# Keys and values of the recurrence turned as 32x32 squares on VectorE, each square carried to its place by a transfer inside SBUF

## The chip, the cores and the metric

The kernel runs on one core of a Trainium2 chip. The metric is the device time of one launch in microseconds (us), the median of several runs. All data are float32. The engines named below are TensorE (PE; its weight loads are shown apart as PEld), VectorE (DVE), ScalarE (ACT), GpSimd (POOL) and the queue engine SyncE (SP), which issues the DMA transfers here.

## The reference

The model is a two-layer block (feed-forward, a pooling and gated recurrence mixer, feed-forward) and then a second block with two mixers. The change lies in the first mixer of the second block, a linear recurrence over tokens with a matrix state per head. It is run over 512 tokens (256 of context, 256 of the input) in both directions, with 16 heads of 64:

```python
def wkv_scan(r, w, k, v, kk, a, s0, reverse):
    def step(S, inp):
        r_t, w_t, k_t, v_t, kk_t, a_t = inp
        sa = jnp.einsum("bhvk,bhk->bhv", S, kk_t)
        S = (S * w_t[:, :, None, :]
             - sa[..., None] * (kk_t * a_t)[:, :, None, :]
             + v_t[..., None] * k_t[:, :, None, :])
        return S, jnp.einsum("bhvk,bhk->bhv", S, r_t)
    s_fin, o = lax.scan(step, s0, xs, reverse=reverse)
```

## The kernel before

Features lie along the 128 partitions and tokens along the row. Weights stream from HBM through a ring of five slots of 1 MB, loaded by SP. After the first block and the projections of the second comes the recurrence, called the scan here, from about 1554 to 2047 us of the profiled span, and after it the output product, an attention mixer and the store.

The scan treats two heads at a time (a pair, 8 pairs, 128 features) and both directions at once. A pair has 8 steps of 64 tokens (`CHUNK`) in each direction. One **turn** q holds two steps in two directions, so four blocks u = (jj, d); a pair has four turns, named g = 0 to 3, and there are 32 turns. In a turn the products inside the blocks are computed (`first_gram`, `stacked_gram`), a 64x64 triangular matrix is inverted for each block by doubling in levels 1 to 5 (`lower_product` on PE, `mask_lower` on DVE, `next_inverse` on PE, `take_inverse` on ACT), and the state of the turn before is carried on with two steps k and k + 1, where k = 2(q - 1) (`state_product`, `take_z`, `solve`, `take_u`, `out_and_state`, `take_o`, `update_state`). Each engine has its own list of these steps, written out by hand in a loop over q, and executes it in order. Semaphores tie the lists together. The side work of a pair (norms, decays, gates) stands at fixed places of its turns, and POOL prepares the next pair meanwhile (`direction`).

Keys and values lie as feature by token. The state update and the output need them as token by feature. So in each turn PE transposes the four blocks of `bk` (128 rows each: 64 of betas and 64 of keys) in `turned_bk` (L1297) and four blocks of values in `turned_v` (L1315), into two PSUM banks; ACT copies these to `bk_t` and to the upper 64 partitions of `uv` (`take_turned_bk`, L1964, `take_turned_v`, L1969). The lower 64 partitions of `uv` are written by `take_u` (L1980). For the direction that runs backward ACT first writes a reversed copy of the values, `v_rev` (L1919), once for a pair. The readers are:

- the tile `kv` (L1369, in `side(q, "kv")`): values with the masked gram matrix, in turn q itself, which needs `uv`'s values of turn q;
- `out_and_state` (L1423, L1427, L1432), in turn q + 1 for the blocks of turn q, which needs `bk_t` and `uv`. Its last product counts up `os_full`.

`bk_t` and `uv` are double-buffered by the parity of q. The lines to follow in the trace: L1287 is `stacked_gram`, at whose first product a turn is counted here as begun; L1327 is `lower_product`, L1338 and L1340 are `next_inverse`, L1399 `state_product`, L1411 `solve`; on ACT L1957 and L1959 are `take_inverse`; on DVE L2763 is `mask_lower`, L2781 `take_z`, L2790, L2792 and L2793 `update_state`, L2753 to L2757 `begin_inverse`, L2697 `sum_decays`. On SP L976 are the weight loads before the scan, L993 those behind it and L996 the stores of the result. SP issues nothing between the load at the end of the projections and the first load for the output product.

## Time and profile before

| | |
|---|---|
| time of the kernel, median of 3 runs | 2393.3 us (2391.81 to 2393.4) |
| time of the profiled execution | 2391.25 us |
| its span in the profile | 2389.2 us |
| PE busy | 2357.6 us, 99% |
| DVE busy | 1526.6 us, 64% |
| ACT busy | 558.5 us, 23% |
| POOL busy | 419.0 us, 18% |
| first and last `stacked_gram` of the 32 turns | 1554.40 and 2035.73 us |

The profile is of one execution. Its span lies 2.05 us below that execution's time, and that time 2.05 us below the median. A row of a timeline says: start, duration, engine, line, operation, what is written and read, how many instructions are merged, and in brackets how long the engine sat idle before and whom it waited for. A float32 product shows as two matmul rows, so `x8` is four products. The granted clock of TensorE is 1.00 in all windows of the scan, its upper level of 2.4 GHz.

### The profile page before, as it was taken

How to read it: one execution, taken by the hardware profiler on the slowest of the kernel's cores; microseconds unless marked ns; L12 is line 12 of the kernel's file. 1: busy time of each engine (PE TensorE's matmuls, PEld its weight loads, DVE VectorE, ACT ScalarE, POOL GpSimd, SP SyncE). 2: the span in 40 equal slices, each digit the busy share in tenths (PEclk: the TensorE clock that was granted, in tenths of full speed). 3: DMA queues.
4: the chain of work that ended last, by engine and by line, in shares of the span. 5: the costliest groups of instructions: out<-in, count | busy, mean ns of one | idle time of the engine just before them, and what ended most of it. 6: DMA issues, size and time to landing. Idle time of an engine off the chain costs nothing.

```text
span 2389.2 us, 54476 instructions
## 1 busy us (share of the span) xinstructions
PE 2357.6 (99%) x24052; PEld 2057.5 (86%) x24052; DVE 1526.6 (64%) x2964; ACT 558.5 (23%) x1289; POOL 419.0 (18%) x483
## 2 busy tenths in 40 slices
PE   8999999999999999999999999999999999999999
PEld 8999888899999998889999888488888888556558
DVE  7886674488778766744987887255555554147652
ACT  2101030111011010301111111245555554132341
POOL 1111000112011100001223320234444440100000
PEclk9999999999999999999999999999999999999999
DMA  7555544445545554545454322000000001212111
GB/s 282 185 180 193 190 178 153 165 161 205 197 162 193 178 194 176 184 151 179 176 193 162 112 80 71 1 3 3 3 3 3 3 3 38 89 53 88 53 53 71
DMA packets 40427, 285.03 MB, mean 119 GB/s; under 512 B 4544, under 2 KB 5744, under 8 KB 6272
## 3 DMA queue, kind: packets, MB, share of 16 engines
q1 hardware_dynamic: 36000, 252.83, 29.6%
q0 software_dynamic: 4192, 28.72, 3.3%
q8 instruction: 190, 3.11, 0.5%
q14 instruction: 45, 0.37, 0.0%
HBM read 280.48 MB, written 1.05 MB: 118 GB/s over the span
## 4 chain that ended last, share of the span: by engine, by line
PE 96%; DVE 2%; ACT 2%; issue 0%; DMA 0%; POOL 0%; SPq 0%; DVEq 0%; ACTq 0%; POOLq 0%
PE psum L696 27%; PE psum L1039 21%; PE psum L1100 12%; PE psum L1208 6%; PE psum L714 5%; PE psum L1338 4%; PE psum L1327 3%; PE psum L1340 2%; PE psum L1287 1%; PE psum L1427 1%; ACT arena L1957 1%; PE psum L1010 1%; PE psum L1274 1%; PE psum L1297 1%; PE psum L1411 1%; PE psum L1355 1%
## 5 line engine op out<-in xcount | busy, mean ns | idle before, releaser
L696 PE MATMUL psum<-arena,ring 128*128 128x256 f32 (+1 forms) x2864 | 675.2, 395 | 8.3 <-ACT arena L1735 8.0
L696 PEld LDWEIGHTS psum<-arena,ring 128*128 128x128 f32 x2864 | 541.8, 190 | 129.7 <-issue 56.5
L1039 PE MATMUL psum<-arena 128*128 128x128 f32 x2560 | 325.0, 275 | 0.0
L1039 PEld LDWEIGHTS psum<-arena 128*128 128x128 f32 x2560 | 305.1, 192 | 0.0
L1039 PE MATMUL psum<-arena,ring 128*128 128x128 f32 x1920 | 253.6, 275 | 0.0
L1039 PEld LDWEIGHTS psum<-arena,ring 128*128 128x128 f32 x1920 | 233.9, 192 | 0.2
L2348 DVE TENSOR_TENSOR arena<-ring 128x1024 f32<-128x1024 f32 x136 | 171.1, 1258 | 38.6 <-PE psum L1100 34.7
L1100 PE MATMUL psum<-arena 128*128 128x128 f32 x1408 | 184.6, 275 | 0.0
L1100 PEld LDWEIGHTS psum<-arena 128*128 128x128 f32 x1408 | 170.7, 192 | 0.0
L2370 DVE SCALAR_TENSOR_TENSOR arena<-arena 128x256 f32<-128x256 f32 x336 | 164.1, 530 | 5.2
L1338 PE MATMUL psum<-arena 64*64 64x64 f32 x2560 | 158.5, 223 | 0.9 <-DVE arena L2763 0.7
L2763 DVE TENSOR_TENSOR arena<-psum,arena 128x256 f32<-128x256 f32 x160 | 67.8, 424 | 140.2 <-PE psum L1327 139.4
L1338 PEld LDWEIGHTS psum<-arena 64*64 64x64 f32 x2560 | 138.4, 133 | 13.5 <-issue 9.2
L1100 PE MATMUL psum<-arena,ring 128*128 128x128 f32 x1056 | 146.0, 275 | 0.0
L714 PE MATMUL psum<-arena,ring 128*128 128x512 f32 (+1 forms) x336 | 138.0, 555 | 1.1 <-DVE arena L2904 1.1
L1340 PE MATMUL psum<-arena 64*64 64x64 f32 x2048 | 131.9, 218 | 0.0
L1100 PEld LDWEIGHTS psum<-arena,ring 128*128 128x128 f32 x1056 | 131.5, 192 | 0.1
L1760 ACT ACTIVATE arena<-arena 128x256 f32<-128x256 f32 x88 | 36.8, 418 | 370.1 <-DVE arena L2486 343.7
L1327 PE MATMUL psum<-arena 64*64 64x64 f32 x2560 | 113.4, 221 | 9.0 <-ACT arena L1957 9.0
L1340 PEld LDWEIGHTS psum<-arena 64*64 64x64 f32 x2048 | 119.6, 135 | 0.0
L1327 PEld LDWEIGHTS psum<-arena 64*64 64x64 f32 x2560 | 94.8, 134 | 20.5 <-ACT arena L1957 13.7
L1957 ACT ACTIVATE arena<-psum 128x512 f32<-128x512 f32 x128 | 76.4, 597 | 147.6 <-PE psum L1340 147.6
(343 smaller groups left out, 3373.1 us busy)
## 6 DMA issues: line engine op xcount, KB each, us to landing
ring<-in_weights SPq DMA_DIRECT2D x238, 1024.0 KB, 4.8
arena<-in_ada POOLq DMA_DIRECT2D x24, 1024.0 KB, 5.4
arena<-in_const POOLq DMA_DIRECT2D x1, 1312.0 KB, 6.4
arena<-in_x SPq DMA_DIRECT2D x1, 1024.0 KB, 4.8
ring<-in_weights SPq DMA_DIRECT2D x2, 512.0 KB, 6.7
arena<-in_ctx POOLq DMA_DIRECT2D x1, 1024.0 KB, 7.5
arena<-in_lora POOLq DMA_DIRECT2D x1, 1024.0 KB, 5.2
out<-arena SPq DMA_DIRECT2D x8, 128.0 KB, 1.9
```

Of the source, the lines that this page charges most:

```text
L696: mm = self.nc.tensor.matmul(out, self.ring[:, slot % RING, i * P:(i + 1) * P], rhs, start=(kc == 0), stop=(kc == len(moving) - 1))
L714: mm = self.nc.tensor.matmul(out, self.ring[:, slot % RING, i * P:(i + 1) * P], rhs, start=start, stop=stop)
L1039: mm = nc.tensor.matmul(bank[:, n * P:(n + 1) * P], left[:, kind, pair, :], right[:, pair, :], start=(n == 0 and pair == 0), stop=(n == la ...
L1100: mm = nc.tensor.matmul(out_[name][:, n * P:(n + 1) * P], left[:, kind, place, :], right[:, pair, :], start=(n == 0 and pair == 0), stop=( ...
L1208: mm = nc.tensor.matmul(out_[:, n * T:(n + 1) * T], left[:, kind, pair, :], right[:, pair, :], start=(n == 0 and pair == 0), stop=(closes ...
L1327: mm = mm_(ps_t[b][halves[h], u, :], lt_all[halves[h], b, u, :], xy[halves[h], b, 0, u, :], start=True, stop=True)
L1338: mm = mm_(ps_xy[b][halves[h], 1, u, :], t_, y_, start=True, stop=True)
L1340: mm = mm_(ps_xy[b][halves[h], 0, u, :], y_, t_, start=True, stop=True)
L1957: ins = nc.scalar.activation(xy[:, b, :, :, :], ps_xy[b], ACT.Copy)
L2348: link(tt(sum_[:, S1:S3 + 1, :], w[:, W22:W11 + 1, :], w[:, W21:W21 + 1, :].to_broadcast([P, 2, QUADS * P]), ALU.add))
L2370: ins = stt(sum_, ada_[:, b, kc, :], weight, sum_, ALU.mult, ALU.add)
L2763: tt(t_low[:, b, :, :], ps_t[b], mask(f"below{level}"), ALU.mult).then_inc(s.t_masked[b], 1)
```

## The change

`turned_bk`, `turned_v` and their copies on ACT go, and `reverse_values` with its buffer. In their place DVE turns squares of 32x32 within a row of partitions (`turn_squares`), and SP carries each row of squares with a transfer from SBUF to SBUF to the partitions where it belongs. For this the layout of `bk_t` and `uv` changes: the block index u is now innermost, so that one partition's row of a square (32 columns, 4 blocks) is contiguous, 512 bytes; every reader and `take_u` now step over four elements (16 bytes) along the features. The reversed direction is read with a negative step. One buffer `squares_turned` holds six groups of squares, four for `bk` and two for the values.

```diff
-    bk_t = second.take(2, 4, P)
-    uv = second.take(2, 4, P)
+    bk_t = second.take(2, P, 4)
+    uv = second.take(2, P, 4)
+    squares_turned = Arena(arena, second.at).take(6, SQUARE, 4)
...
+            for q in range(TURNS):
+                b, n = q % 2, q // 2 + 1
+                if q >= 2:
+                    sp.wait_ge(s.bk_landed[b], 16 * 16 * (n - 1))
+                    sp.wait_ge(s.v_landed[b], 8 * 16 * (n - 1))
+                sp.wait_ge(s.squares_turned, q + 1)
+                if q >= 2:
+                    sp.wait_ge(s.os_full, 2 * q - 2)
+                for c in range(6):
+                    rows = slice(c % 4 * SQUARE + c // 4 * CHUNK, c % 4 * SQUARE + c // 4 * CHUNK + SQUARE)
+                    dst, landed = (bk_t, s.bk_landed) if c < 4 else (uv, s.v_landed)
+                    for f in range(P // SQUARE):
+                        cols = slice(f * SQUARE, (f + 1) * SQUARE)
+                        sp.dma_start(dst[rows, b, cols, :], squares_turned[cols, c, :, :]).then_inc(landed[b], 16)
+                for i in range(2):
+                    if q == TURNS - GROUPS + 1 + i:
+                        load_b(i)
+            for i in range(2, SECOND_B_SLOTS):
+                load_b(i)
...
                     if kind == "kv":
                         pe.wait_ge(s.gram_taken, q + 1)
-                        pe.wait_ge(s.act_taken, SCAN.taken(("v_turned", q)))
+                        pe.wait_ge(s.v_landed[q % 2], 8 * 16 * (q // 2 + 1))
...
-                                         uv[HEAD:P, q % 2, u, h * HEAD:(h + 1) * HEAD], start=True, stop=True)
+                                         uv[HEAD:P, q % 2, h * HEAD:(h + 1) * HEAD, u], start=True, stop=True)
...
                 pe.wait_ge(s.u_taken, k + 1)
+                if jj == 0:
+                    pe.wait_ge(s.bk_landed[par], 16 * 16 * (q // 2 + 1))
...
-                        mm = mm_(ps_s[halves[h], d, :], bk_t[:, par, 2 * jj + d, cols], uv[:, par, 2 * jj + d, cols],
+                        mm = mm_(ps_s[halves[h], d, :], bk_t[:, par, cols, 2 * jj + d], uv[:, par, cols, 2 * jj + d],
...
                 next_inverse(q, 3)
-                turned_bk(q)
-                turned_v(q)
                 lower_product(q, 4)
...
+            def turn_squares(q):
+                pair, g = divmod(q, GROUPS)
+                if g == 0:
+                    dve.wait_ge(s.pair_ready, pairs_ready(pair, 1))
+                if q >= 1:
+                    dve.wait_ge(s.bk_landed[(q - 1) % 2], 16 * 16 * ((q - 1) // 2 + 1))
+                    dve.wait_ge(s.v_landed[(q - 1) % 2], 8 * 16 * ((q - 1) // 2 + 1))
+                stream, at = g // 2, g % 2 * 2 * CHUNK
+                for d in range(2):
+                    nc.vector.transpose(
+                        squares_turned[:, 0:4, :, d::2].rearrange("p c j u -> p u c j"),
+                        bk[:, pair % 2, d, 2 * g:2 * g + 2, :].rearrange("p u (c j) -> p u c j", j=SQUARE))
+                    values = rkv[:, 2 * DC + pair, stream * T:(stream + 1) * T]
+                    values = (values if d == 0 else values[:, ::-1])[:, at:at + 2 * CHUNK]
+                    ins = nc.vector.transpose(
+                        squares_turned[:, 4:6, :, d::2].rearrange("p c j u -> p u c j"),
+                        values.rearrange("p (u c j) -> p u c j", u=2, c=2))
+                ins.then_inc(s.squares_turned, 1)
...
             begin_inverse(1)
+            dve.wait_ge(s.lora_in, 4)
+            turn_squares(0)
...
                 if q % GROUPS == 0 and q // GROUPS + 1 < PAIRS:
                     sum_decays(q // GROUPS + 1)
+                elif ahead:
+                    turn_squares(q + 1)
                 if ahead:
                     mask_lower(q + 1, 2)
                 if k >= 0:
                     update_state(k + 1)
+                if q % GROUPS == 0 and q // GROUPS + 1 < PAIRS:
+                    turn_squares(q + 1)
```

PE, turn 5 (the second turn of the second pair), from the end of level 3 to the first step of the state. Before: L1340 is the end of `next_inverse`, L1297 and L1315 the two transposes, L1327 `lower_product`, L1423 the start of `out_and_state`.

```order
L1340 MATMUL psum<-arena 64x64
L1297 MATMUL psum<-arena,ring 128x128 [waits act_taken]
L1297 MATMUL psum<-arena,ring 128x128 x3
L1315 MATMUL psum<-arena 128x128 [waits act_taken]
L1315 MATMUL psum<-arena,ring 128x128
L1315 MATMUL psum<-arena 128x128
L1315 MATMUL psum<-arena,ring 128x128
L1327 MATMUL psum<-arena 64x64 [waits xy_taken_1]
L1327 MATMUL psum<-arena 64x64 x7
L1423 MATMUL psum<-ring,arena 64x64 [waits u_taken]
L1423 MATMUL psum<-ring,arena 64x64 x3
```

The same place after the change. Its line numbers are those of the changed kernel: L1342 is `next_inverse`, L1329 `lower_product`, L1427, L1431 and L1436 are `out_and_state`.

```order
L1342 MATMUL psum<-arena 64x64
L1329 MATMUL psum<-arena 64x64 [waits xy_taken_1]
L1329 MATMUL psum<-arena 64x64 x7
L1427 MATMUL psum<-ring,arena 64x64 [waits bk_landed_0,u_taken]
L1427 MATMUL psum<-ring,arena 64x64 x3
L1431 MATMUL psum<-arena 64x64 x4
L1436 MATMUL psum<-arena 64x64 x4
```

The eight transposes are gone, `lower_product` stands directly behind `next_inverse`, and `out_and_state` waits for the keys' transfers as well.

DVE, the second half of turn 5. Before: L2763 is `mask_lower`, L2781 `take_z(k + 1)`, L2792 and L2793 `update_state(k + 1)`.

```order
L2763 TENSOR_TENSOR arena<-psum,arena 128x256 [waits t_full_1]
L2781 TENSOR_TENSOR arena<-psum,arena 128x128 [waits z_full]
L2763 TENSOR_TENSOR arena<-psum,arena 128x256 [waits t_full_0]
L2792 TENSOR_TENSOR arena<-psum,arena 128x128 [waits o_taken]
L2793 TENSOR_TENSOR arena<-arena 128x128 [waits dve_chain]
```

The same place after the change; L2750 and L2755 turn the squares of turn 6.

```order
L2764 TENSOR_TENSOR arena<-psum,arena 128x256 [waits t_full_1]
L2782 TENSOR_TENSOR arena<-psum,arena 128x128 [waits z_full]
L2750 STREAM_TRANSPOSE arena<-ring 128x2x128 [waits v_landed_1,bk_landed_1]
L2755 STREAM_TRANSPOSE arena<-arena 128x2x64
L2750 STREAM_TRANSPOSE arena<-ring 128x2x128
L2755 STREAM_TRANSPOSE arena<-arena 128x2x64
L2764 TENSOR_TENSOR arena<-psum,arena 128x256 [waits t_full_0]
L2793 TENSOR_TENSOR arena<-psum,arena 128x128 [waits o_taken]
L2794 TENSOR_TENSOR arena<-arena 128x128 [waits dve_chain]
```

Four transposes stand between `take_z` and the next `mask_lower`, and wait until all transfers of turn 5 have landed. In turns with g = 0 they stand behind `update_state(k + 1)` instead.

SP, after the change, from the first loads through two turns of the scan; L980 are the weight loads, L1017 the new transfers of 32 partitions by 128 elements. Before, the load of the first slot behind the scan follows directly on the `x214`.

```order
L980 DMA ring<-in_weights 128x2048 [waits slot_used] x214
L1017 DMA arena<-arena 32x128 [waits squares_turned]
L1017 DMA arena<-arena 32x128 x23
L1017 DMA arena<-arena 32x128 [waits squares_turned]
L1017 DMA arena<-arena 32x128 x23
L1017 DMA arena<-arena 32x128 [waits squares_turned,os_full,v_landed_0,bk_landed_0]
L1017 DMA arena<-arena 32x128 x23
```

Each of the 32 turns has 24 transfers in a row; from turn 2 on the first of them waits for `os_full`, which guards the buffer that is written over.

## Rows read from the trace of the kernel before

**Rows 1.** The page, busy time by engine and the chain that ended last.

```profile
PE 2357.6 (99%) x24052; PEld 2057.5 (86%) x24052; DVE 1526.6 (64%) x2964; ACT 558.5 (23%) x1289; POOL 419.0 (18%) x483
...
PE 96%; DVE 2%; ACT 2%; issue 0%; DMA 0%; POOL 0%; SPq 0%; DVEq 0%; ACTq 0%; POOLq 0%
```

**Rows 2.** Windows, turns 4 to 7: us, then busy PE, PEld, DVE, ACT, POOL.

```profile
1615.34:1631.23 15.89, 15.67 (x399) 13.91 (x396) 9.41 (x19) 8.41 (x19) 1.27 (x1) 1.00 0.01 3
1631.23:1647.31 16.08, 15.86 (x384) 13.45 (x381) 8.75 (x19) 9.18 (x22) 13.33 (x12) 1.00 0.02 4
1647.31:1662.35 15.04, 14.79 (x387) 13.81 (x384) 8.29 (x17) 6.97 (x16) 9.06 (x7) 1.00 0.02 4
1662.35:1678.25 15.90, 15.68 (x399) 13.92 (x396) 7.70 (x19) 7.09 (x16) 4.12 (x3) 1.00 0.01 3
sum 62.91, PE 62.00 PEld 55.08 DVE 34.16 ACT 31.66 POOL 27.78; mean PE 15.50 PEld 13.77 DVE 8.54 ACT 7.92 POOL 6.95
```

**Rows 3.** Timeline of turn 5 around the transposes: start, duration, engine.

```profile
1633.68 0.66 PE L1297 MATMUL psum<-arena,ring 128*128 128x128 f32 x4
...
1634.71 0.68 PE L1327 MATMUL psum<-arena 64*64 64x64 f32 x16
...
1633.79 0.60 ACT L1957 ACTIVATE arena<-psum 128x512 f32<-128x512 f32 x1 [0.22 <-PE psum L1340]
```

**Rows 4.** Waits of PE in the scan: us in total, times, longest.

```profile
PE psum L1327 <- ACT arena L1957: 9.0, 34, 0.8
```

**Rows 5.** Timeline of DVE, turns 3 to 6, the gaps and three durations.

```profile
1612.08 0.29 DVE L2793 TENSOR_TENSOR arena<-arena 128x128 f32<-128x128 f32 x1
...
1627.71 0.17 DVE L2790 MEMSET arena<- 128x128 f32 x1 [0.77 <-ACT arena L1992]
1630.87 0.29 DVE L2781 TENSOR_TENSOR arena<-psum,arena 128x128 f32<-128x128 f32 x1 [3.00 <-PE psum L1399]
...
1633.34 0.42 DVE L2757 TENSOR_TENSOR arena<-arena 128x256 f32<-128x256 f32 x1
...
1642.56 0.42 DVE L2763 TENSOR_TENSOR arena<-psum,arena 128x256 f32<-128x256 f32 x1 [2.10 <-PE psum L1327]
...
1649.86 1.50 DVE L2757 TENSOR_TENSOR arena<-arena 128x256 f32<-128x256 f32 x1
```

**Rows 6.** Timeline of PE in turn 5, readers of the turned tiles.

```profile
1635.55 0.45 PE L1427 MATMUL psum<-arena 128*64 128x64 f32 x8
1635.83 0.40 PE L1432 MATMUL psum<-arena 128*64 128x64 f32 x8
1636.17 1.12 PE L1387 MATMUL psum<-arena 128*128 128x512 f32 x2
...
1641.27 0.27 PE L1369 MATMUL psum<-arena 64*64 64x64 f32 x1
...
1641.69 0.27 PE L1327 MATMUL psum<-arena 64*64 64x64 f32 x1
...
1643.30 0.34 PE L1338 MATMUL psum<-arena 64*64 64x64 f32 x4
```

**Rows 7.** SP's issues: timeline at the start; durations in ns; landing in us.

```profile
2.78 1.99 SPq L976 DMA_DIRECT2D ring<-in_weights  x4
...
L976 SPq DMA_DIRECT2D ring<-in_weights x214: 327/328/1092, 2.8 to 1475.0; - x107
...
L996 SPq DMA_DIRECT2D out<-arena x8: 332/340/456, 2371.8 to 2386.9; - x8
...
DMA to landing us min/median/max: 1.9/1.9/4.0
```

**Rows 8.** Timeline of turn 0, DVE and PE.

```profile
1553.78 0.42 DVE L2757 TENSOR_TENSOR arena<-arena 128x256 f32<-128x256 f32 x1
...
1555.49 0.34 PE L1338 MATMUL psum<-arena 64*64 64x64 f32 x4
...
1564.86 0.27 PE L1369 MATMUL psum<-arena 64*64 64x64 f32 x1
```

More of the change, by code:

```diff
@@ L89 @@
 STACK_BANKS = (2, 5)
+SQUARE = 32
 DA_HEADS = 8
@@ L405 @@
 SECOND_A = second_a_order()
-PLACES = ("bk_turned", "v_turned", "middle", "kv", "end")
+PLACES = ("middle", "kv", "end")
 def scan_tiles(q, place):
@@ L414, in scan_tiles @@
     inside, ahead, behind = 0 <= pair < PAIRS, pair + 1 < PAIRS, pair >= 1
-    if place in ("bk_turned", "v_turned", "kv"):
+    if place == "kv":
         return [(place, q, "act")] if inside else []
@@ L583, in __init__ @@
         self.y_ready = new("y_ready")
-        self.reversed_ready = new("reversed_ready")
+        self.squares_turned = new("squares_turned")
+        self.bk_landed = [new(f"bk_landed_{b}") for b in range(2)]
+        self.v_landed = [new(f"v_landed_{b}") for b in range(2)]
         self.out_squared = new("out_squared")
@@ L838, in build @@
     bk, ar = by_pair[:, :, 0], by_pair[:, :, 1]
-    v_rev = v_part.take(2, CHUNK + T2)
     prod = v_part.take(STEPS, CHUNK + 1), second.take(STEPS, CHUNK + 1)
@@ L976, in _, with load_b @@
                 sp.dma_start(ring[:, r, :], weights[i]).then_inc(s.slot_landed[r], 16)
-            sp.wait_ge(s.slot_used, RING_AT_REST)
-            for i in range(SECOND_B_SLOTS):
+            def load_b(i):
                 r = (RING_SHIFT + i) % RING
                 if i == 0:
-                    sp.wait_ge(s.act_taken, SCAN.taken(("bk_turned", TURNS - GROUPS - 1)))
+                    sp.wait_ge(s.slot_used, RING_AT_REST)
+                    sp.wait_ge(s.squares_turned, TURNS - GROUPS)
+                    sp.wait_ge(s.stack_full, TURNS - GROUPS)
                 elif i == 1:
@@ L985, in _ @@
                 elif i == 2:
-                    sp.wait_ge(s.act_taken, SCAN.taken(("bk_turned", TURNS - 1)))
+                    sp.wait_ge(s.squares_turned, TURNS)
+                    sp.wait_ge(s.stack_full, TURNS)
                 elif i == 3:
@@ L989, in _ @@
                 elif i == 4:
-                    sp.wait_ge(s.act_taken, SCAN.taken(("v_turned", TURNS - 1)))
+                    sp.wait_ge(s.pair_ready, pairs_ready(PAIRS - 1, 1))
                 else:
@@ L1426, in out_and_state @@
                     for h in range(2):
-                        mm_(ps_o[halves[h], d, :], uv[:, par, 2 * jj + d, h * HEAD:(h + 1) * HEAD],
+                        mm_(ps_o[halves[h], d, :], uv[:, par, h * HEAD:(h + 1) * HEAD, 2 * jj + d],
                             gram_at(par, jj, d, h)[:, CHUNK:], start=False, stop=True)
@@ L1924, in side_head @@
                 n = pair + 1
-                if g == 0 and n < PAIRS:
-                    reverse_values(n)
                 if g == 1 and n < PAIRS:
```

42 lines of the change are left out of this document (1 added, 41 removed).

## The prediction, made before the changed kernel ran

> **What bounds the kernel now.** I read the page's busy times and chain first. PE is busy 99% of the span and holds 96% of the chain [rows 1], so a change pays only where it shortens PE's row of work or costs where it makes PE wait. Then the windows of four turns, one pair of the scan: PE is busy 15.50 of 15.73 us in a mean turn, DVE 8.54, ACT 7.92, POOL 6.95 [rows 2]. The turns last 15.89, 16.08, 15.04 and 15.90 us. DVE and ACT have room, but the room lies in gaps. PE's waits in the scan are small: 9.0 us in all on `take_inverse` [rows 4]. Last the timelines around the places that the change touches.
>
> **PE's transposes, removed.** In turn 5 the first transpose starts at 1633.68 and `lower_product` of level 4 at 1634.71, so eight transposes take 1.03 us [rows 3]. They are not worth 1.03 us, since they cover a wait: `lower_product` needs ACT's `take_inverse`, which runs from 1633.79 to 1634.39. PE follows such a release by about 0.05 us, so the product starts at 1634.44, which is 0.27 us earlier. What is late next is thus ACT's copy. For the 31 turns after the first that is 31 x 0.27 = 8.4 us. The copies on ACT (about 1.2 us in a turn) and the reversed values go as well; ACT is idle there, so they count as nothing.
>
> **DVE's transposes, added.** A turn adds two of 256 and two of 128 elements a partition. No transpose stands in the trace. The nearest rows are element by element operations inside SBUF, 0.42 us for 256 and 0.29 us for 128 [rows 5], so 2 x (0.42 + 0.29) = 1.42 us; I take this, and twice it, 2.84, as the upper bound. A faster one gains nothing, as they are hidden. In turns with g = 1 to 3 they stand in the gap of 2.10 us before `mask_lower` at 1642.56, in those with g = 0 behind the `MEMSET` at 1627.71, ahead of a gap of 3.00 us [rows 5]. Both hold 1.42 us. At 2.84 us the first gap is 0.74 us too short; the mask's reader, `next_inverse`, starts at 1643.30, 0.32 us after the mask ends, so 0.4 us is left in 24 turns, 10 us. POOL's work next door can do the same: one 256-element operation took 1.50 us instead of 0.42 [rows 5].
>
> **SP's transfers, added.** 24 issues in a row and a landing. The trace has no transfer of 32 rows. Issues of 128 rows take 0.33 us each, alone [rows 7]; four back to back at the start take 1.99 us, 0.50 each. The last store needs 1.9 us from issue to landing. I take 0.41 us between two issues, the middle, as a quarter of the rows should not be dearer than 128: 23 x 0.41 + 1.9 = 11.3 us, and 0.1 us for the wake-up makes 11.4. The bounds are 23 x 0.33 + 2.0 = 9.6 and 23 x 0.50 + 2.0 = 13.5 us.
>
> The time available is read from two places. In a turn with g = 0 the squares are ready at 1627.71 + 0.17 + 1.42 = 1629.30, and `kv` (L1369), which needs the values, which are issued last, starts at 1641.27 [rows 5, 6]; less the 0.27 us gained that is 11.7 us. In the other turns SP waits for `os_full`, the end of `out_and_state(k + 1)`, that is about 1643.30, not for the squares; from there to the next `kv` is a turn less 2.03 us (1643.30 - 1641.27). With the shortest usual turn, 15.04 - 0.27, it is 12.7 us. So 11.4 us fits both, by 0.3 us in the first. DVE's next transposes want the landing about 0.8 us before `kv` does; the gap's spare 0.68 us takes most of that. Queued behind a late landing on DVE would be `mask_lower(q + 1, 2)` and `update_state`; behind a late one on PE all of the scan.
>
> **Once, at the start.** `turn_squares(0)` stands between `begin_inverse(1)`, done at 1554.20, and `mask_lower(0, 3)`. The latter then ends at 1554.20 + 1.42 + 0.43 = 1556.05, and `next_inverse`, at 1555.49 before, starts 0.6 us late. The transfers land at 1554.20 + 1.42 + 11.4 = 1567.0, and `kv` of turn 0 started at 1564.86 [rows 8]. This costs 2.2 us in all, once; bounds 0.4 and 4.3 us by the two prices of the transfers. The loads for the output product are issued later, behind the squares of turns 29 to 31, but the first is needed only after the scan; I cost this at nothing.
>
> **Strided reads, changed.** `kv` reads `uv`, and the last two products of `out_and_state` read `uv` and `bk_t`, over a step of 16 bytes. In time on PE these are 0.42 us (1641.27 to 1641.69) and twice 0.28 + 0.34 us (1635.55, 1635.83, 1636.17) [rows 6], 1.66 us in a turn. No row has an operand with a step, apart from tiny ones. The lower bound is no cost (the rows as they are), the upper a doubling, 1.66 x 32 = 53 us. The nearest row is the same product with a step of one, so I take nothing, and keep 53 us for a rival. `take_u` writes with this step too: 0.42 us for two copies, on ACT, which has room.
>
> This is the one place where the Trainium skill speaks against the change. Its page "SBUF — State Buffer", section "Door 1: The DMA port swizzle", says that SBUF has lines of 16 bytes, that at least two hits on a line are needed for full bandwidth, and yet that four float32 can be stepped over for free. Taken by its first half each read here meets a new line; taken by its second it costs nothing. No run here shows it. The page "DMA: Bandwidth & Descriptors", section "Bandwidth", calls transfers under 64 KB dominated by descriptors; these have 16 KB.
>
> **The sum.** -8.4 + 2.2 = -6.2 us. The profiled execution of 2391.25 us becomes 2385.0; against the median, 2.05 us higher, 2387.1. I forecast 2387.0 us.
>
> **Rivals.**
>
> 1. *SP can't issue fast enough.* The scan then follows a new ring: 24 transfers, `kv`, `out_and_state`, `os_full`, 24 transfers. For it: the four back-to-back issues at 0.50 us. Against: an issue alone takes 0.33 us. At 0.50 us the 13.5 us miss the 11.7 us after each g = 0 by 1.8, and the 12.7 us of the short turn by 0.8: 2.6 x 8 pairs = 21 us, at the start 4.3 instead of 2.2, so -8.4 + 21 + 4.3 = +17 us, 2410. It costs from 0.42 us on, since 23 x 0.42 + 2.0 = 11.7, and by about 0.44 us it has eaten the gain. At 0.65 us a turn needs 16.95 + 2.03 = 19.0 us, and the total would be near 2510.
>
> 2. *The strided operands are read slowly.* -6.2 + 53 = +47, 2440 us; at half that price 2414. It decides from 0.2 us in a turn on. It needs no queue to fail, since PE has nothing to hide it behind; for it speaks that these reads were all packed before, against it only that a float32 product of 64 columns is no faster than its neighbours. The skill's line rule, first half, is this rival; by its second half it falls.
>
> 3. *DVE's squares are dearer*, by themselves or beside POOL, which works 13.33 of 16.08 us in a turn with g = 1 [rows 2]: -6.2 + 10 = +4, 2397 us.
>
> 4. *The gain is larger*, if the freed 1.03 us could be used in full: only if ACT's copy were not the next wait, which row and order exclude.
>
> **Chances.** The forecast, with covers that hold, 40%: its own range is 2384 to 2395. Rival 1, 23%; rival 2, 28%; rival 3, 9%. A measurement of this kernel can tell about 0.2%, 4.8 us, from no change. Of the forecast's 40%, 31 lie below 2388.5 and 9 within; rivals 1 and 3 bring 8 more within, and 1 for a lucky case below. So faster 0.32, same 0.17, slower 0.51: the likeliest single case is a small gain, but the cases on the other side hold more together. The range reaches over rival 2 and most of rival 1: 2383 to 2450. It leaves out a deeper failure of SP's pace (12%) and a few per cent below.
>
> **What would show it.** Right: no L1297 and L1315; the turns of a pair 0.27 us shorter; the groups of `kv` and `out_and_state` with the same spacing; SP's issues at 0.41 us or less; DVE's four transposes 1.42 us and no wait for a DMA on PE. Rival 1: PE's waits name the new transfers, all turns equally long, SP busy through. Rival 2: PE busy as before, but 0.28 and 0.34 us of L1427 and L1432 grown, and the loads too, with no wait behind it. Rival 3: DVE's transposes over 2.1 us, or PE waiting for `mask_lower`. What would make the prediction wrong at once is a pace above 0.42 us or any price on the step of 16 bytes.

## The result and the profile after

The changed kernel takes **2623.09 us** (median, 2621.86 to 2624.62), the kernel before 2393.35: a ratio of 1.0965, 95% interval 1.0952 to 1.0978. The forecast was 2387.0, a small gain, with a range from 2383 to 2450. The kernel became slower instead, and its time lies 236 us above the forecast.

The page comes first: busy times, the granted clock over 40 slices, and each engine's part in the chain that ended last.

```profile
PE 2428.3 (93%) x23796; PEld 2119.7 (81%) x23796; DVE 1568.1 (60%) x3091; ACT 531.0 (20%) x1217; POOL 416.4 (16%) x483
...
PEclk9999999999999999999999998888888888899999
...
PE 74%; SPq 18%; DMA 2%; issue 2%; DVE 2%; ACT 1%; POOL 0%; DVEq 0%; ACTq 0%; POOLq 0%
```

PE had 96% of the chain [rows 1] and now has 74%; of the 22 points that it lost, 18 went to SP's queue (SPq). The clock row falls in the slices of the scan only (the eights). The next rows are the windows of turns 4 to 7, to be held against [rows 2]. A row gives the length in us, then the busy time of PE, PEld, DVE, ACT and POOL, the granted clock, the DMA share and GB/s:

```profile
1646.25:1668.12 21.87, 17.13 (x391) 15.26 (x388) 10.96 (x23) 7.18 (x16) 1.28 (x1) 0.92 0.08 18
1668.12:1693.72 25.60, 18.63 (x376) 15.74 (x373) 10.32 (x23) 8.43 (x20) 21.93 (x18) 0.80 0.09 21
1693.72:1715.31 21.59, 16.49 (x379) 15.43 (x376) 8.52 (x21) 6.24 (x14) 0.00 (x0) 0.92 0.09 19
1715.31:1738.85 23.54, 17.81 (x391) 15.94 (x389) 9.26 (x23) 6.35 (x14) 4.11 (x3) 0.85 0.09 20
```

Four turns last 92.60 us, where they were 62.91. Over all 32, from the first `stacked_gram` (1553.80) to the last (2256.74), a turn has 22.68 us in the mean, against 15.53 before. That is 31 x 7.15 = 222 of the 230 us; most of the rest lies in the last turn and the last steps of the state behind it. DMA works 8 to 9% of the time, so the engines that move the bytes are not what is short.

Next the waits in the scan (us in total, how often, the longest), first of PE, whose largest was 9.0 us before [rows 4], and of DVE, then of SP:

```profile
PE psum L1371 <- DMA arena<-arena: 137.3, 31, 7.3
DVE arena L2750 <- DMA arena<-arena: 131.7, 24, 7.2
...
SPq L1008 <- DVE arena L2755: 111.3, 30, 7.0
...
SPq L1011 <- PE psum L1436: 46.9, 24, 2.1
```

PE's `kv` (L1371) and DVE's next squares (L2750) wait for the landing, and SP waits for DVE's squares and for PE's `out_and_state` (L1436) before it may issue again: a ring. One passage of it in turn 6, from the timeline (start, duration, engine, line, what; in brackets the idle time before and what ended it):

```profile
1707.48 0.64 DVE L2750 STREAM_TRANSPOSE arena<-ring 128x256 f32<-128x256 f32 x1 [5.34 <-DMA arena<-arena]
1707.49 0.67 PEld L1371 LDWEIGHTS psum<-arena 64*64 64x64 f32 x12 [4.30 <-issue]
1707.52 0.78 PE L1371 MATMUL psum<-arena 64*64 64x64 f32 x10 [4.19 <-DMA arena<-arena]
...
1709.87 0.75 PE L1431 MATMUL psum<-arena 128*64 128x64 f32 x8
...
1710.40 0.69 PE L1436 MATMUL psum<-arena 128*64 128x64 f32 x8
```

And SP's issues of L1017 (durations in ns, minimum, median, maximum; under it the time to landing):

```profile
L1017 SPq DMA_DIRECT2D arena<-arena x768: 507/591/1880, 1555.1 to 2269.4; - x192
...
DMA to landing us min/median/max: 1.7/1.8/3.7
```

From the starts of the 768 issues: within a row of 24, two neighbours lie 0.633 us apart in the median, 0.717 in the mean. So the first and the last of 24 lie 16.50 us apart in the mean; 1.85 us later the last has landed, and 4.16 us after that SP issues the next row's first (the way back). The sum, 22.5 us, is the turn. The window that the forecast read from the trace of before was 11.7 us.

The way back is not the same in all turns. In six turns with g = 0, where DVE's squares stand behind `update_state` and SP waits for them, it is 5.6 to 5.9 us. In the usual other turns it is 3.85 us, with a granted clock of 0.50 (the lower level, 1.2 GHz) from the landing to the next issue. In the two turns where the clock was 1.00 there, it is 3.21 us. Two such stretches, both from turns with g = 3, from the last landing to SP's next issue:

```profile
2002.12:2005.97 3.85, 3.71 (x59) 3.51 (x61) 1.98 (x5) 0.44 (x2) 0.00 (x0) 0.50 0.00 0
1911.72:1914.93 3.21, 3.21 (x74) 3.04 (x71) 2.02 (x5) 1.55 (x6) 1.23 (x1) 1.00 0.01 3
```

So the usual way back is 0.64 us longer at the lower clock. Whether the clock fell because PE waits is asked further down.

### The profile page after: what moved, and what is told of

It is laid out like the page before. It is cut to its first block, busy times and chain, and to the rows that moved or that the text cites. A ratio compares the mean times of both kernels' runs of the same rounds, so it can differ in the third digit from the quotient of the medians.

```text
span 2619.8 us, 54905 instructions
## 1 busy us (share of the span) xinstructions
PE 2428.3 (93%) x23796; PEld 2119.7 (81%) x23796; DVE 1568.1 (60%) x3091; ACT 531.0 (20%) x1217; POOL 416.4 (16%) x483
## 4 chain that ended last, share of the span: by engine, by line
PE 74%; SPq 18%; DMA 2%; issue 2%; DVE 2%; ACT 1%; POOL 0%; DVEq 0%; ACTq 0%; POOLq 0%
PE psum L699 25%; PE psum L1068 19%; SPq L1017 18%; PE psum L1129 11%; PE psum L1237 5%; PE psum L717 5%; DMA arena<-arena 2%; PE psum L1371 1%; PE psum L1329 1%; PE psum L1039 1%; PE psum L1427 1%; PE psum L1431 1%; PE psum L1589 1%; PE psum L1631 1%; PE psum L1436 1%
## 5 line engine op out<-in xcount | busy, mean ns | idle before, releaser
L1340 PE MATMUL psum<-arena 64*64 64x64 f32 x2560 | 174.6, 236 | 0.9 <-DVE arena L2764 0.9
L1371 PE MATMUL psum<-arena 64*64 64x64 f32 x512 | 37.1, 297 | 137.3 <-DMA arena<-arena 137.3
L1340 PEld LDWEIGHTS psum<-arena 64*64 64x64 f32 x2560 | 150.6, 143 | 15.7 <-issue 9.9
L1329 PE MATMUL psum<-arena 64*64 64x64 f32 x2560 | 132.5, 236 | 31.5 <-ACT arena L1952 31.5
L1342 PE MATMUL psum<-arena 64*64 64x64 f32 x2048 | 146.7, 233 | 0.0
L1329 PEld LDWEIGHTS psum<-arena 64*64 64x64 f32 x2560 | 112.1, 147 | 41.9 <-ACT arena L1952 39.5
L1371 PEld LDWEIGHTS psum<-arena 64*64 64x64 f32 x512 | 31.1, 186 | 140.7 <-issue 140.7
L1342 PEld LDWEIGHTS psum<-arena 64*64 64x64 f32 x2048 | 131.9, 149 | 0.0
```

The source lines that it names most:

```text
L1329: mm = mm_(ps_t[b][halves[h], u, :], lt_all[halves[h], b, u, :], xy[halves[h], b, 0, u, :], start=True, stop=True)
L1340: mm = mm_(ps_xy[b][halves[h], 1, u, :], t_, y_, start=True, stop=True)
L1342: mm = mm_(ps_xy[b][halves[h], 0, u, :], y_, t_, start=True, stop=True)
L1371: mm = mm_(out_[halves[h], u * HEAD:(u + 1) * HEAD], gram_at(q % 2, jj, d, h)[HEAD:P, 0:CHUNK], uv[HEAD:P, q % 2, h * HEAD:(h + 1) * HEAD, ...
```

## Experiments

All ratios are to the kernel before, run on the same chip beside each (2391.4 to 2392.2 us).

**One part of the change at a time.** First the layout alone, in the kernel before:

```diff
-    bk_t = second.take(2, 4, P)
-    uv = second.take(2, 4, P)
+    bk_t = second.take(2, P, 4)
+    uv = second.take(2, P, 4)
...
-    uv[HEAD:P, q % 2, u, h * HEAD:(h + 1) * HEAD]
+    uv[HEAD:P, q % 2, h * HEAD:(h + 1) * HEAD, u]
```

> The kernel before, with one part of the change alone: the buffers bk_t and uv are laid out with the four units innermost, so that PE reads them, and ACT writes them, over a step of 16 bytes. The transposes stay on PE, and no transfers are added. Theory A, that SP's transfers alone lengthened the turn from 15.5 to 22.7 us and that the granted clock fell as a consequence: the time stays within 5 us of 2393, since the step costs nothing. Theory B, that the step has a price of its own: in the trace of the changed kernel the three groups of reads were wider than before (about 0.16 us each for the first two products of the output, 0.14 for the third, 0.1 to 0.2 for kv, twice or once a turn), which makes 0.8 to 1.2 us in a turn and 25 to 40 us in 32, so 2418 to 2433 us, with PE busy throughout and the granted clock at 1.00. Theory C, that the step is most of the loss and the transfers only wait for a slower PE: over 2500 us.

Measured: **2441.91 us**, 1.0213 (1.0196 to 1.0230), so +50.5 us. Theory B had the mechanism, but its 25 to 40 us were too low. The groups of the three readers (busy us, mean ns of one), first of the kernel before, then of this one:

```profile
L1427 PE MATMUL psum<-arena 128*64 128x64 f32 x512 | 28.9, 234 | 0.0
...
L1432 PE MATMUL psum<-arena 128*64 128x64 f32 x512 | 25.8, 222 | 0.0
L1369 PE MATMUL psum<-arena 64*64 64x64 f32 x512 | 25.4, 221 | 0.1
```

```profile
L1427 PE MATMUL psum<-arena 128*64 128x64 f32 x512 | 44.3, 294 | 0.0
L1432 PE MATMUL psum<-arena 128*64 128x64 f32 x512 | 44.0, 305 | 0.0
L1369 PE MATMUL psum<-arena 64*64 64x64 f32 x512 | 40.1, 293 | 0.0
```

15.4 + 18.2 + 14.7 = 48.3 us, nearly all of it. PE stays 99% busy, and no wait of PE grows by more than 0.2 us in total: this cost doesn't show as a wait.

Then the whole change with half of its transfers (`for f in range(0, P // SQUARE, 2)`, and the counts that are waited for halved):

> The changed kernel with 12 transfers to a turn in place of 24: half of the squares are not moved, so half of the turned keys and values are left out; everything else, DVE's transposes and the step of 16 bytes too, is as changed. Theory A, SP's pace: the measured mean of 0.72 us from issue to issue makes 11 x 0.72 + 1.8 = 9.7 us for 12, which fits the 11.7 us that the shortest window holds, so the ring of transfers and products opens; the turns fall from 22.7 to 15.3 us plus the price of the step (0 to 1.2 us), the total is between 2385 and 2425 us, the granted clock in the scan returns to 1.00, and PE's wait for the transfers (137 us) is nearly gone. Rival: the transfers are late because of where they start (the wait for the output product and the landing), not because of how many they are: then a turn loses only what it gains in the middle, and stays above 18 us, over 2470 us in all.

Measured: **2434.80 us**, 1.0180 (1.0165 to 1.0196). The usual turns of a pair are 17.14, 17.31, 16.19 and 17.14 us, where the kernel with the step alone has 17.41, 17.57, 16.46 and 17.41: in each 0.27 us less, which is the gain that the forecast read from [rows 3]. The granted clock is 1.00 in the four windows of these turns. The first:

```profile
1619.17:1636.31 17.14, 16.23 (x391) 14.54 (x389) 10.96 (x23) 7.18 (x16) 1.29 (x1) 1.00 0.06 12
```

Taken away in this order, the parts are: the step +50.5, PE's transposes removed and the first dozen of transfers added -7.1 (2434.80 less 2441.91), and the second dozen of transfers +188.3 us. Each is the difference of two neighbouring runs, so that they add up to the whole by construction. Another order gives other parts, as the packed kernel further down shows.

> The changed kernel with 18 transfers to a turn (a quarter of the squares is not moved, and that part of the turned keys and values is left out). With 24 a turn takes 22.7 us, with 12 the ring is open and a turn takes 17.1 (of which 1.5 are the step, as the kernel before with the step alone showed). Theory A, a ring of SP's issues at a mean 0.72 us each: the turn is 22.7 - 6 x 0.72 = 18.4 us, so 31 x (18.4 - 17.14) = 39 us over the kernel with 12, about 2474 us, and up to 15 us less if the granted clock recovers; the point at which it stops to cost lies at 16 to 17 transfers. Rival, a threshold instead of a line (the lower granted clock is what makes the turn long, and it is either there or not): the time is either that of 12, 2435, or over 2550 us.

Measured: **2498.90 us**, 1.0448 (1.0434 to 1.0462). It is not the one value or the other of the rival: the time lies between, but 25 us above the expected 2474. From SP's issues: first to last 12.03 us (17 x 0.71, as expected), the last landing 2.68 us later in place of 1.85, then 4.07, together 18.8 us. What the expectation left out is that the landing of the last transfer can be late too, 2.9 to 3.7 us in 17 of 32 turns; with 24 transfers it was late in one. Six turns have the length that they have with 12 transfers (17.14 or 16.2 us), so there the transfers came in time.

**What an issue costs.** The block of spare transfers, in the kernel before:

```diff
+            def square_moved(i):
+                sp.dma_start(there[rows(i % 4), cols(i // 4)], here[rows(i // 4), cols(i % 4)]).then_inc(s.tried, 16)
...
+            def from_hbm(i):
+                sp.dma_start(there[rows(i % 4), cols(i // 4)], weights[i][rows(i % 4), cols(i // 4)]).then_inc(s.tried, 16)
```

> The kernel before, with spare transfers issued by SP in the turns 1 to 27 of the scan, whose data nobody reads; nine forms in blocks of three turns, 16 issues back to back in a turn (4 for the widest form), each form on a source line of its own: a square of 32 rows by 512 bytes to other rows and to the same rows, a short one of 32 rows by 128 bytes, 128 rows by 128 bytes, 128 rows by 512 bytes, 32 rows by 512 bytes from HBM, 128 rows by 128 bytes from HBM, 32 rows by 512 bytes to HBM, and 16 rows by 1 KB. Theory A, the price of an issue depends on where its source and destination lie: from SBUF to SBUF about 0.59 us whatever its size, from HBM about 0.33 us with 0.50 back to back, as at the start of the kernel before. Theory B, it grows with the number of pieces: 128 rows cost clearly over 32 rows of the same form. Theory C, crossing from rows to other rows costs more than staying on the same rows. In every case the kernel's own time stays within 15 us of 2393, as SP is idle in the scan, and PE's granted clock at 1.00.

Measured: 2392.02 us in one run, with a granted clock of 1.00 in the scan, so the spare transfers cost the kernel nothing. Theory A holds, with 0.42 us for HBM back to back in place of 0.50. The forms (ns, as above): a square to other rows (L992), a square on its rows (L995), 128 rows by 128 bytes (L1001), 128 rows by 512 bytes (L1004), a square from HBM (L1007), to HBM (L1013).

```profile
L992 SPq DMA_DIRECT2D arena<-arena x48: 507/591/1539, 1571.7 to 1611.9; - x48
...
L995 SPq DMA_DIRECT2D arena<-arena x48: 507/591/1738, 1616.1 to 1659.0; - x48
...
L1001 SPq DMA_DIRECT2D arena<-arena x48: 464/602/1692, 1710.9 to 1753.0; - x48
...
L1004 SPq DMA_DIRECT2D arena<-arena x12: 464/601/602, 1757.8 to 1790.7; - x12
...
L1007 SPq DMA_DIRECT2D arena<-in_weights x48: 310/422/1895, 1804.8 to 1845.7; - x48
...
L1013 SPq DMA_DIRECT2D scratch_out<-arena x48: 302/422/1449, 1899.6 to 1939.3; - x48
```

Inside SBUF, rows, bytes and whether partitions are crossed change next to nothing (a square of 4 KB 0.59 us, 128 rows of 64 KB 0.60). What counts is whether one end lies in HBM (0.42) or none (0.59).

> The changed kernel with the buffers bk_t and uv packed again, as in the kernel before, so that PE reads without a step; the same 24 transfers to a turn, each in runs of 128 bytes in place of 512 (128 pieces of 128 bytes, 16 KB as before), and DVE's transposes write packed. Theory A, the ring is SP's issues: it still holds, and loses only the price of the step that lies in it (kv and one output product, 0.2 to 0.8 us a turn): 2595 to 2620 us, if an issue costs the same for four times as many pieces. Theory B, an issue is paid by its pieces: 0.59 us becomes well over 1 us, a turn over 35 us, over 3000 us in all. Theory C, the step is the main cause: below 2500 us.

Measured: **2624.05 us**, 1.0974 (1.0958 to 1.0991). Four times as many pieces cost an issue 602 ns in place of 591. Theory A holds in its mechanism, not in its size: the packed reads should have shortened the ring, but the time is the changed kernel's. SP's first to last grew to 16.81 us (0.3 lost) and the rest fell to 5.8 us, 3.90 and 1.87 (0.2 won).

The way back tells why so little was won. Where the granted clock is 0.50 it is 3.68 us in a usual turn, against 3.85 with the step: there the step costs only 0.17 us. Where the clock is 1.00, in two turns, it is 2.24 us against 3.21:

```profile
2187.51:2189.75 2.24, 2.10 (x61) 2.00 (x63) 1.58 (x5) 0.44 (x2) 0.00 (x0) 1.00 0.00 0
```

So in the changed kernel the step's 50 us do not come on top of the ring: without the step, the 24 direct transfers alone make it as slow.

The longest issues stood out. In the changed kernel 83 took over 0.9 us, and all of them overlap in time with a packet of 16 KB from an instruction queue, itself 0.9 to 1.5 us long; of the 685 shorter ones 79 do. In the scan there are 93 such packets (packets, MB, share):

```profile
q8 instruction: 93, 1.52, 0.9%
```

That is only a coincidence in a trace, so the same transfers were run where no other engine works:

> The kernel before, and behind its last store, where no other engine works, four blocks of 48 transfers of 32 rows by 512 bytes each, of which nobody reads the data: SP from SBUF to SBUF, SP from HBM to SBUF, ACT's queue from SBUF to SBUF alone, then SP's and ACT's both at once. Theory A, the long issues (1.0 to 1.9 us, 2 to 3 in a turn of the scan) come from PE's instruction fetches: here no issue is over 0.7 us and the mean start to start is 0.63 us, 0.46 for HBM. Rival, they belong to SP's own queue: as many long ones as in the scan, 6 or 7 in 48, mean 0.70 to 0.75. On both at once, theory B: each queue keeps 0.63 us, so that two queues halve the time of 24 transfers; rival: they share one path and each slows to 1.2 us. The whole adds 48 x (0.63 + 0.46 + 0.63 + 0.63) + 8 = 121 us, 2510 us in all.

The kernel took 2514.41 us in one run, where 2510 were expected. The 48 issues of each block (L2159 has two blocks), and below them the packets of the instruction queue in the whole stretch:

```profile
L1005 SPq DMA_DIRECT2D ring<-ring x48: 586/590/592, 2392.4 to 2422.2; - x48
...
L1008 SPq DMA_DIRECT2D ring<-in_weights x48: 310/421/442, 2423.9 to 2445.9; - x48
...
L1012 SPq DMA_DIRECT2D ring<-ring x48: 518/599/828, 2479.9 to 2510.2; - x48
...
L2159 ACTq DMA_DIRECT2D ring<-ring x96: 515/612/613, 2447.7 to 2509.9; - x96
...
q14 instruction: 2, 0.02, 0.0%
```

The median is that of the scan, and the long ones are gone (592 ns at most against 1539). So they come from what the other engines do in the scan. The instruction packets are the one traffic found beside them; no run took these away alone, so that they are the cause is likely and not shown. The mean start to start is 0.633 us, against 0.717 in the scan: the long ones add 23 x 0.084 = 1.9 us to a turn. SP's and ACT's queues at once (L1012 with the second half of L2159) keep 0.64 us each, so the price belongs to the issuing queue.

**Is it the number of issues?** If so, fewer and cheaper ones do away with the 188 us, though the bytes are moved twice, out to HBM in 8 transfers and back in 2:

```diff
-                        sp.dma_start(dst[rows, b, cols, :], squares_turned[cols, c, :, :]).then_inc(landed[b], 16)
+                    sp.dma_start(v_out[b, :, cols, :].rearrange("(c i) j u -> i c j u", c=2), squares_turned[cols, 4:6, :, :])
...
+                sp.dma_start(uv[CHUNK:P, b, :, :], v_out[b]).then_inc(s.v_landed[b], 16)
```

> The changed kernel with DVE's transposes and the step of 16 bytes as changed, but the squares go to a buffer in HBM in 8 stores to a turn (32 rows each, pieces of 512 bytes) and from there to bk_t and uv in 2 loads: 10 issues in place of 24, all with one end in HBM, which in the block of spare transfers took 0.42 us each back to back against 0.59 from SBUF to SBUF. Theory A, the number of issues and their price make the ring: stores 8 x 0.46 = 3.7, landing 1.6, loads 0.9 and 2.0, together 8.2 us, fit the window, so the time is that of the kernel with 12 transfers, 2430 to 2440 us (the step's 50 us less the 8.4 us of PE's removed transposes). Rival, the bytes and pieces make it (twice the traffic): the wait of PE for the load stays, over 2500 us.

Measured: **2434.72 us**, 1.0177 (1.0163 to 1.0191), to 0.1 us the time of the kernel with 12 transfers, and with all of the data. In its scan neither PE nor DVE waits for a transfer. One more thing differs: SP starts the 8 stores without waiting for `os_full`, since they don't write over `bk_t` and `uv`, and DVE waits for the stores alone. That part of the ring is open whatever the count, so this run does not separate the number of issues from where they start. The kernel with 12 transfers does: it keeps the starting point, and its ring opens because the transfers are fewer. Now the step too is taken away, with 4 stores and 6 loads:

> As the kernel by way of HBM, but with bk_t and uv packed as in the kernel before, so that PE and ACT work without the step: 4 stores to a turn (32 rows, 768 pieces of 128 bytes each, 96 KB) and 6 loads (32 rows, 128 pieces of 512 bytes, 64 KB). Theory A, both causes taken away leave the change's gain: 2391.4 - 8.4 + 1 to 3 us once at the start = 2384 to 2386 us, the turns of a pair 0.27 us shorter than before. Rival 1, the small pieces are slow: 3072 pieces of 128 bytes to a turn need more than the 11.7 us window together with the loads; then PE waits for the loads and the time is over 2400 us. Rival 2, DVE's transposes of 2.0 us cost something of their own: 2388 to 2400 us without a wait for a transfer on PE.

Measured: **2389.28 us**, 0.9988 (0.9979 to 0.9997): a small gain, 4 us short of Theory A. Against the packed kernel with 24 direct transfers (2624.05) it is 235 us: in this order the transfers cost all and the step nothing. Its turns tell why 4 us are missing. Most are 0.27 us shorter, as 15.63 for 15.90. Those with g = 2 are 15.27 for 15.04, and turn 1 is 17.19 for 15.65. In the turns with g = 2, PE now waits for DVE's mask (L2763 before, L2767 here). The waits for it in the whole scan, before and after:

```profile
PE psum L1338 <- DVE arena L2763: 0.7, 1, 0.7
```

```profile
PE psum L1344 <- DVE arena L2767: 4.1, 8, 0.7
```

In turn 1 a single wait of 1.76 us for ACT, which loads a table there (the wait was 0.74 us before), is followed by five microseconds at a granted clock of 0.66, a stretch partly at the lower level of 1.2 GHz; the two wide products in it take 2.08 us in place of 1.12:

```profile
1570.69:1575.00 4.31, 2.55 (x61) 2.29 (x58) 2.98 (x6) 4.17 (x8) 0.75 (x1) 1.00 0.34 65
1575.00:1580.00 5.00, 5.00 (x73) 3.31 (x75) 2.56 (x5) 1.53 (x4) 4.81 (x5) 0.66 0.19 57
```

The first of the two, the wait for the mask, has a cure:

```diff
-                mask_stack(q, 0)
-                mask_lower(q, 4)
+                if q % GROUPS == 2:
+                    mask_lower(q, 4)
+                    mask_stack(q, 0)
+                else:
+                    mask_stack(q, 0)
+                    mask_lower(q, 4)
```

> The packed kernel by way of HBM with one change of DVE's order: in the turns with g = 2 mask_lower of level 4 stands ahead of the first mask_stack, not behind it. There POOL's work slows begin_inverse (1.36 and 1.49 us in place of 0.69 and 0.42), so that the mask ended at 1653.13 and PE waited 0.52 us for it, in 8 turns 4.1 us in all; in the kernel before PE's eight transposes covered this wait, so the gain of 0.27 us in a turn became a loss of 0.23 in these turns (15.04 to 15.27 us). Theory A: the mask's place is the cause. It starts 0.6 us earlier, the wait goes, these turns fall to 14.8 us and the time by about 4 us, to 2385 us, 0.3% under the kernel before. Rival: the wait only moves to mask_stack's readers or to update_state, and the time stays at 2389.

Measured: **2385.15 us**, 0.9970 (0.9959 to 0.9982); the usual turns with g = 2 fall to 14.69 us, and of the 8 waits one is left, which the kernel before has too. This version is faster than both kernels, than the one before by 7 us, 0.3%.

**DVE's part, and the step's size.**

> The kernel before with DVE's four transposes of a turn added, at the places of the changed kernel and into a packed buffer that nobody reads; PE's transposes and ACT's copies stay. It asks for the price of DVE's part alone. Theory A, hidden in DVE's gaps, as forecast: 2391 to 2393 us, with 0.42 and 0.27 us for the two kinds (1.4 us in a turn), plus at most 0.6 us once at the start. Rival, it delays mask_lower in the turns where POOL works beside DVE: 2395 to 2405 us, and PE's waits name L2763's line with several us.

Measured: **2391.64 us**, 0.9999 (0.9990 to 1.0008). The squares are hidden here, where nothing waits for their landing; 28 of the 32 turns have them. With a packed output they take 413 and 269 ns, 1.36 us in a turn; in the changed kernel, where they write over the step, 627 and 392, or 2.04.

> The kernel before with bk_t and uv laid out over a step of 8 bytes (two units innermost) in place of 16, for PE's reads and ACT's writes alike; nothing else is changed. The step of 16 bytes cost 50.5 us. Theory A, that what counts is how many of the operand's elements lie in one line of 16 bytes (the Trainium skill, page SBUF - State Buffer, section Door 1: The DMA port swizzle, holds two hits on a line to be enough): no cost, 2391 us. Theory B, any step but one costs the same: 2442 us. Theory C, the cost grows with the step: between, about 2415.

Measured: **2395.13 us**, 1.0011 (1.0002 to 1.0020), +2.9 us. PE's three means are 237, 224 and 222 ns, 1 to 3 ns more than packed; ACT's copy of 512 elements is 636 ns, where it was 596 packed and 1099 over 16 bytes. So nearly all of the price comes between 8 and 16 bytes; 12 were not tried. The Trainium skill (SBUF — State Buffer, Door 1: The DMA port swizzle) asks for at least two hits on a line of 16 bytes for full bandwidth, and with that the trace agrees; its reading that four float32 can be stepped over for free is refuted here by 50 us.

> The kernel before with the step of 16 bytes in bk_t alone, which is the stationary operand of one of the three groups (L1432) and is written by one of ACT's copies; uv stays packed. With both stepped that group's product rose from 222 to 305 ns in the mean and the three groups cost 15.4, 18.2 and 14.7 us. Theory A, one stepped operand of a product costs as much as two, whichever it is: 15 to 18 us, 2407 to 2410 us. Theory B, the two operands add up: 8 to 10 us, 2400 to 2402. Theory C, a stepped stationary operand is hidden behind the product before it: within 3 us of 2392.

Measured: **2408.02 us**, 1.0065 (1.0050 to 1.0080), +15.8 us, Theory A. The group L1432 goes from 25.8 us to 41.1 with one stepped operand and to 44.0 with two; the prices of two operands of one product don't add up.

**The clock.** It fell to 0.80 to 0.92 in the changed kernel's turns. Is it the cause of the long turns or a consequence? PE gets products that nobody reads, ahead of its wait:

```diff
+                        for i in range(FILLERS):
+                            filler = gram_at(q % 2, 0, 0, 0)[HEAD:P, 0:CHUNK]
+                            mm_(out_[halves[i % 2], 0:HEAD], filler, filler, start=True, stop=True)
                         pe.wait_ge(s.v_landed[q % 2], 8 * 16 * (q // 2 + 1))
```

> The changed kernel, with 128 small products on PE in each turn ahead of its wait for the transfers, written to the tile of kv, which the real products overwrite: about 3.4 us in a turn, while PE waited 4.4 us there in the mean. The granted clock in the scan was 0.86. Theory A, the lower clock follows from PE's waits and costs little by itself, since the ring is SP's: the clock rises towards 1.00, and the time stays between 2600 and 2640 us. Rival, the lower clock is what makes the turns long: with it back at 1.00 the time falls below 2560 us.

Measured: **2678.63 us**, 1.1197 (1.1182 to 1.1213), clock 1.00, usual turns of 24.6 us. No theory met this: I had mis-sized the filling, 7.5 us in a turn and not 3.4, so that PE was the bound (96% busy in the scan). Repeated with 60:

> The changed kernel with 60 in place of 128 small products on PE in each turn ahead of its wait for the transfers. The 128 took 7.5 us in a turn (24.6 against 17.1), 58 ns each, so that PE and not SP was the bound, and that run says nothing of the clock's price; 60 are 3.5 us, and PE's work in a turn 20.6 us, under the ring's 22.5. Theory A, the lower clock (0.86) follows from PE's waits and costs little: the clock rises to 0.95 or more, the turn stays within 0.6 us of 22.6, the time between 2600 and 2640 us. Rival, the lower clock makes up 1.5 us or more of the 5.6 us that a turn is longer than with 12 transfers: with the clock back the time falls to 2575 us or less. A second rival, more instructions on PE mean more fetches that hold SP's issues up: the time rises by the same share as the long issues, to 2650 us.

Measured: **2636.80 us**, 1.1032 (1.1014 to 1.1051). The clock rose, but less than expected. The same 690 us of the scan and 100 us of it, first of the changed kernel, then of this one:

```profile
1560.00:2250.00 690.00, 527.72 (x11469) 470.07 (x11469) 291.74 (x672) 212.05 (x470) 187.61 (x151) 0.87 0.09 22
1660.00:1760.00 100.00, 77.28 (x1665) 68.57 (x1667) 41.14 (x97) 31.91 (x70) 28.60 (x23) 0.86 0.08 18
```

```profile
1560.00:2250.00 690.00, 613.20 (x14940) 558.04 (x14942) 289.65 (x666) 210.60 (x465) 187.69 (x151) 0.92 0.09 22
1660.00:1760.00 100.00, 91.08 (x2286) 82.60 (x2284) 43.97 (x100) 31.90 (x71) 28.68 (x23) 0.97 0.09 20
```

So the clock follows PE's waits: it is 1.00 with 128 products and 0.92 in the scan with 60. But the mean from one row of issues to the next is 22.8 us, for 22.5, and nothing speaks for the rival in which the clock makes up 1.5 us or more of a turn. The way back shows its size directly. In this run too it is 3.7 to 3.8 us in the usual turns at the lower level and 3.1 in six turns where the clock was higher (three more of these were longer, for reasons not found), so the clock is worth some 0.6 us a turn. By an estimate from the two rows of the changed kernel, 31 x 0.64, that is up to 20 us of its 230. Here the gain of a few turns doesn't show in the time. The last landing came 2.19 us behind its issue in place of 1.85, and 32 x 0.34 = 11 us is as much as the 10.4 us between the spans of the two profiled executions. There were 141 packets of the instruction queues for 111, which fits the second rival in direction.

## Why the prediction was wrong, by its steps

- **PE's transposes removed, -8.4 us: right, where the ring is open.** 0.27 us in a turn, seven us in all. One thing was missed: in turns with g = 2 DVE's mask, slowed by POOL, ended late enough for PE's transposes to cover a wait of 0.52 us for it too. With the step this doesn't show (16.46 us become 16.19); without it, it cost 4 us. "What is late next" has to be asked for each kind of turn, not for one.
- **DVE's transposes, 1.42 us, hidden: right, where the ring is open.** 1.36 us packed, 2.04 with the step, both in the gaps. Rival 3 falls. In the changed kernel their late place in the turns with g = 0 lies in the ring, and six ways back are about 2 us longer.
- **SP's transfers: the step of the prediction that failed.** I took 0.41 us from issue to issue with bounds of 0.33 and 0.50, "as a quarter of the rows should not be dearer than 128". Measured are 0.633 without disturbance and 0.717 in the scan, so 16.5 + 1.85 us against a window of 11.7. Both rows that I took the price from [rows 7] have one end in HBM. Rows and bytes, on which I had argued, hardly enter, and the kind of the ends does. The range was narrow for the wrong reason: two rows of one kind bound nothing for another kind.
- **The ring of rival 1 was right in kind and short in size.** It was named, with 23% and a price at 0.65 us of 19.0 us a turn. Measured: 22.5. Of the 3.5 us, 1.5 are the pace (16.5 for 14.95 us) and 2.1 the way back, 4.16 us where 2.03 stood. The turns at a full clock and a packed layout (2.24 us), at a full clock with the step (3.21) and at the lower clock (3.85) give the way back piece by piece: 0.2 for wake-ups, 1.0 for the step, 0.6 for the clock, and 0.4 in the mean for DVE's squares behind g = 0. The first two of these rest on two turns of a run each. The deeper failure of SP's pace, left out of the range with 12%, is what came.
- **Strided reads, taken as nothing: wrong.** Alone it is +50.5 us, almost the doubling that stood as the upper bound (53), on PE and without any wait. The "nearest row" was the same product with a step of one, which says nothing on the step. This was rival 2. Each of the two errors would have turned the sign by itself; I priced them as alternatives, and both came. Their prices don't add: with the ring closed the kernel is as slow packed (2624.05) as with the step (2623.09).
- **Once at the start, 2.2 us:** it can't be told apart in the ring; in the packed kernel by way of HBM the first turns cost 1.4 us together, for a reason not forecast (the clock after ACT's table load).
- **The sum.** -7.1 + 50.5 + 188.3 = +231.7 us on 2391.4 gives the measured 2623.1 by construction and checks nothing. In the other order the parts are -2.8 (the packed kernel by way of HBM, against the one before), +234.8 (24 direct transfers in its place) and -1.0 (the step). What does check is the ring: 16.50 + 1.85 + 4.16 = 22.5 us, where the turns last 22.68. The pieces of the 4.16 us are read from traces; no run changed them one by one.

## What to carry to other kernels

Price a transfer by what its two ends are, from a row that has the same ends, and count issues before bytes: a row of many small transfers costs its number times SP's pace, and once waits close a ring, each turn lasts as long as the whole ring. Ask of a new layout whether the innermost step of a float32 operand stays within 8 bytes, since a step that PE pays appears in no list of waits. Parts of a change that are measured alone need not add up, since a ring hides what it does not wait for. When work that covered a wait is removed, look for the next wait in each kind of turn.

## What was not expected of the hardware

- An issue from SBUF to SBUF takes 0.59 us on SP (0.61 on ACT's queue) back to back, for 4 to 64 KB and for pieces of 128 or 512 bytes alike; with one end in HBM it takes 0.42 on SP, measured at 16 KB. Two queues hardly slow each other (0.64 us start to start each, 0.633 alone).
- Beside the other engines' work 1 issue in 9 takes 0.9 to 1.9 us, and every one overlaps with a 16 KB packet of an instruction queue; at the kernel's end, with only two packets of 8 KB in 118 us, no issue is over 0.61 us while one queue works alone.
- A detour through HBM, in a turn 4 stores of 768 pieces of 128 bytes each and 6 loads, was free, where 24 direct transfers in the same packed layout cost 235 us.
- A float32 operand read or written with a step of 16 bytes: the state's product from 222 to 305 ns and its weight load from 138 to 216, ACT's copy from 596 to 1099, DVE's transpose from 413 to 627. With a step of 8 bytes it is 2 ns for the product and the load and 40 for the copy. In the way back the step cost 0.97 us at the full clock and 0.17 at the lower one.
- One wait of 1.8 us on PE was followed by 5 us at a granted clock of 0.66. In the ring, with waits of 4 us in each turn, the clock was 0.87 in the scan and 0.50 just behind most waits.
